# The first stage of a two-block transformer kernel: scale tiles ahead of the first products, shift tiles behind them

## The reference

```
mod = (silu(c) @ ada_w[0] + ada_b[0]).reshape(3, 3, D)          # shift, scale, gate for each sub-layer
def rms_norm(x, g): return x * rsqrt(mean(x * x) + eps) * g
h = rms_norm(x, g_pre) * (1 + scale) + shift                    # modulate_pre
g_, u = split(h @ w_in, 2)                                      # w_in 1024 x 5632
y = (silu(g_) * u) @ w_out                                      # w_out 2816 x 1024
x = x + 0.5 * gate * rms_norm(y, g_post)
```

## Time and profile before

| | us |
|---|---|
| median of 3 runs | 2181.11 |
| lowest and highest run | 2179.35, 2183.25 |
| profiled execution, its own time | 2186.3 |
| its span | 2184.4 |
| TensorE products busy in it | 2104.6 |

### The profile page before, as it was taken

The page is one execution under the profiler, slowest core; times in us unless marked ns, Lnnn a source line. Parts: engine busy times, 40 slices in busy tenths (PEclk is TensorE's granted clock), DMA queues, the critical chain, the costliest instruction groups (busy, mean ns, idle before and its releaser), DMA issues.

```text
span 2184.4 us, 39484 instructions
## 1 busy us (share of the span) xinstructions
PE 2104.6 (96%) x17016; PEld 2058.6 (94%) x17016; DVE 1586.2 (73%) x1948; ACT 1013.8 (46%) x1097; POOL 199.6 (9%) x333
## 2 busy tenths in 40 slices
PE   5999999999999998899999999999999999999998
PEld 5999999999999998699998999999999899999998
DVE  6887888787757876778888454768898646767655
ACT  3444545445433445644345453346344545336443
POOL 2110101111101101011101000001111000001000
PEclk9999999999879999999999999999999999999999
DMA  8898566995669953058975565446996655544663
GB/s 292 308 345 278 200 214 212 335 342 187 231 223 323 338 198 116 10 191 301 336 269 173 175 198 181 168 169 227 360 362 215 208 184 177 173 163 165 223 214 123
DMA packets 265389, 497.40 MB, mean 228 GB/s; under 512 B 17152, under 2 KB 146560, under 8 KB 264832
## 3 DMA queue, kind: packets, MB, share of 16 engines
q1 hardware_dynamic: 230192, 366.42, 50.2%
q0 software_dynamic: 35024, 128.47, 15.8%
HBM read 491.68 MB, written 1.05 MB: 226 GB/s over the span
## 4 chain that ended last, share of the span: by engine, by line
PE 81%; DVE 11%; ACT 4%; DMA 2%; issue 2%; SPq 0%; DVEq 0%; ACTq 0%
PE PA L505 8%; PE PA L507 8%; PE PA L506 8%; PE PY L505 7%; PE PB L505 7%; PE PY L507 7%; PE PB L507 7%; PE PY L506 7%; PE PB L506 7%; DVE wlo L1363 3%; ACT whi L1004 1%; DVE opA_lo L1452 1%; PE PA L585 1%; PE PA L536 1%; PE PB L901 1%
## 5 line engine op out<-in xcount | busy, mean ns | idle before, releaser
L1363 DVE TENSOR_TENSOR wlo<-raw,whi 128x2048 fp32r<-128x2048 f32 x335 | 768.0, 2302 | 346.2 <-ACT whi L1004 345.1
L1004 ACT ACTIVATE whi<-raw 128x2048 fp32r<-128x2048 f32 x335 | 636.5, 1907 | 493.8 <-DMA raw<-ffn_w_in 198.0
L505 PE MATMUL PY<-opB_hi,whi 128*128 128x256 f32 x1344 | 378.5, 282 | 9.1 <-DVE wlo L1363 8.3
L505 PE MATMUL PA<-opA_hi,whi 128*128 128x256 f32 x1312 | 371.8, 283 | 5.5 <-DVE opA_lo L1413 5.5
L506 PE MATMUL PY<-opB_lo,whi 128*128 128x256 f32 x1344 | 376.7, 280 | 0.0
L507 PE MATMUL PY<-opB_hi,wlo 128*128 128x256 f32 x1344 | 376.7, 280 | 0.0
L507 PE MATMUL PA<-opA_hi,wlo 128*128 128x256 f32 x1312 | 370.0, 282 | 0.0
L506 PE MATMUL PA<-opA_lo,whi 128*128 128x256 f32 x1312 | 369.0, 281 | 0.0
L505 PE MATMUL PB<-opA_hi,whi 128*128 128x256 f32 x1184 | 334.2, 282 | 1.1 <-DVE wlo L1363 1.0
L507 PE MATMUL PB<-opA_hi,wlo 128*128 128x256 f32 x1184 | 333.2, 281 | 0.0
L506 PE MATMUL PB<-opA_lo,whi 128*128 128x256 f32 x1184 | 332.2, 281 | 0.0
(11 more groups left out here) (311 smaller groups left out, 3629.5 us busy)
## 6 DMA issues: line engine op xcount, KB each, us to landing
raw<-ffn_w_in SPq DMA_DIRECT2D x176, 512.0 KB, 5.9
scr<-adat POOLq DMA_DIRECT2D x158, 512.0 KB, 6.4
raw<-w_in SPq DMA_DIRECT2D x144, 512.0 KB, 4.6
raw<-w_ff SPq DMA_DIRECT2D x128, 512.0 KB, 4.9
raw<-ffn_w_out SPq DMA_DIRECT2D x88, 512.0 KB, 5.1
adaw<-adat POOLq DMA_DIRECT2D x82, 512.0 KB, 6.2
raw<-w_branch SPq DMA_DIRECT2D x48, 512.0 KB, 4.6
raw<-a_w_in SPq DMA_DIRECT2D x24, 512.0 KB, 4.7
```

Source lines behind the costliest of these rows:

```text
L505: nc.tensor.matmul(o_, w1, rhs(xh), start=start, stop=False, skip_group_check=True)
L1004: AC(whi[slot][:, 0:w], raw[slot][:, 0:w], ACT.Copy).then_inc(hi_ready, 1)
L1363: TT(wlo[slot][:, 0:w], raw[slot][:, 0:w], whi[slot][:, 0:w].bitcast(F32), ALU.subtract).then_inc(lo_ready, 1)
```

## The change

The sync engine now loads the eight scale tiles first (tile 8 of the table is the first in order, `tile_of`), then chunk 0, x, chunk 1, four shift tiles, chunk 2, four shift tiles, chunk 3. Tiles 6 to 15 in the new order go into buffers of their own in a free area (`first_slab`), each with its own semaphore, so that none waits for a slab. VectorE makes the scale vector after eight tiles, then splits chunk 0, makes the low parts of the operand, splits chunk 1, multiplies four shift tiles and makes their half of the shift columns (mark `00.wide0`), splits chunk 2, and does the same with the other four (`00.wide1`). ScalarE makes all eight high parts before it rounds chunk 1, and rounds chunks 2 and 3 after the squares. TensorE's fillers come after tiles 3 to 8; another eight wait for chunk 0's high part.

`first_zgroups` replaces the two calls of `zgroup` in this stage: chunks 0 and 1 are multiplied with 256 columns, the high part of the operand first and the low part behind it; a block of 32 products with two columns (`shifts`) for chunk 0 stands behind chunk 1, the one for chunk 1 behind chunk 2, and `xnorm` behind that. Chunk 0 is counted as used after its block, chunks 1 and 2 together after the second. Chunks 2 and 3 keep 258 columns. VectorE waits for that count before it evacuates A and B. `ffn_due` of this stage starts its 40 tiles two chunks later and ends at the same place. A memset of GpSimd moves behind the first 16 tiles.

```diff
--- before.py
+++ after.py
@@ -201,7 +201,7 @@
         lo_ready = sem("lo_ready")
         multiplied = sem("multiplied")
         ada_ready = [sem(f"ada_ready{i}") for i in range(SLABS)]
-        first_ready = [sem(f"first_ready{i}") for i in range(SLABS)]
+        first_ready = [sem(f"first_ready{i}") for i in range(16)]
         ada_used = sem("ada_used")
         crow_in = sem("crow_in")
         crow_again = sem("crow_again")
@@ -303,17 +303,25 @@
             [(72 + 8 * b, V("ada_b", 72 + 8 * b, 8)) for b in range(9)] + [(160 + 8 * b, V("b_ada_2", 8 * b, 8)) for b in range(12)]
 
         nsa0 = RUN["nsa"][0]
-        SL = [g % SLABS for g in range(nsa0)] + [g % 2 for g in range(4)] + [(2 + g) % SLABS for g in range(256 - nsa0 - 4)]
+        SL = list(range(SLABS)) + [100 + g for g in range(SLABS, 16)] + [g % SLABS for g in range(16, nsa0)] + [g % 2 for g in range(4)] + [(2 + g) % SLABS for g in range(256 - nsa0 - 4)]
         BEFORE = [max([h for h in range(g) if SL[h] == SL[g]], default=-1) for g in range(256)]
 
         def ffn_due(name, p):
 
-            rn, a_ = RUN[name][1], 3 if name in ("ffn00", "ffn10") else 5
+            rn, a_ = RUN[name][1], 3 if name == "ffn10" else 5
             return min(rn, max(0, p - a_ + 1) * rn // (FFN_AT["in", FFN_STEPS - 1] - a_))
 
         def ff2_due(name, p):
             rn = RUN[name][1]
             return min(rn, max(0, p - 5) * rn // (FF2_AT["out", FF2_STEPS - 2] - 6))
+
+        def first_slab(g):
+
+            return slab[g] if g < SLABS else mix[:, D * (g - SLABS):D * (g - SLABS) + D]
+
+        def tile_of(g):
+
+            return g + 8 if g < 8 else g - 8 if g < 16 else g
 
         def ada_count(g):
             return sum(1 for h in range(16, g + 1) if SL[h] == SL[g])
@@ -391,9 +399,7 @@
             def first_ada(tiles):
 
                 for f in tiles:
-                    if f >= SLABS:
-                        sp.wait_ge(ada_used, f - SLABS + 1)
-                    sp.dma_start(slab[f % SLABS], I["adat"][f]).then_inc(first_ready[f % SLABS], 16)
+                    sp.dma_start(first_slab(f), I["adat"][tile_of(f)]).then_inc(first_ready[f], 16)
 
             def ffn(name, w_in, w_out):
                 c0 = CH[name]
@@ -415,7 +421,9 @@
                         for h in range(2):
                             chunk(p_ + h, src_ffn_in(w_in, j * 256, h))
                             if p_ + h == 0:
-                                first_ada(range(6, 16))
+                                sp.dma_start(x[:], I["x_fm"]).then_inc(x_in, 16)
+                            if p_ + h in (1, 2):
+                                first_ada(range(4 + 4 * (p_ + h), 8 + 4 * (p_ + h)))
                     else:
                         chunk(p_, src_out(w_out, j * 256))
 
@@ -427,8 +435,7 @@
             first_ada(range(0, 2))
             sp.dma_start(vec[:], I["vec"]).then_inc(vec_in, 16)
             sp.dma_start(base[:], I["t_base"]).then_inc(base_in, 16)
-            first_ada(range(2, 6))
-            sp.dma_start(x[:], I["x_fm"]).then_inc(x_in, 16)
+            first_ada(range(2, 8))
             ffn("ffn00", I["ffn_w_in"][0, 0], I["ffn_w_out"][0, 0])
             for n_, g in enumerate(CONV_ORDER):
                 for h in range(2):
@@ -550,6 +557,50 @@
                 for h in range(2):
                     zchunk(c + h, banks, tile, range(4 * h, 4 * h + 4), sub, hook if h == 0 else None)
 
+            def first_zgroups():
+
+                def z(c, banks):
+                    pe.wait_ge(lo_ready, c + 1)
+                    n = T if c < 2 else ZC
+                    for kk in range(4):
+                        k = 4 * (c % 2) + kk
+                        need(pe, "S", f"00.zhi{k}")
+                        for m in range(4):
+                            w_ = slice(tile_ffn_in(kk, m), tile_ffn_in(kk, m) + P)
+                            nc.tensor.matmul(banks[m][:, 0:n], whi[c][:, w_], wide[:, k, 0:n], start=k == 0, stop=False,
+                                             skip_group_check=True)
+                            nc.tensor.matmul(banks[m][:, 0:n], wlo[c][:, w_], wide[:, k, 0:n], start=False, stop=False,
+                                             skip_group_check=True)
+                        need(pe, "V", f"00.zlo{k}")
+                        for m in range(4):
+                            w_ = slice(tile_ffn_in(kk, m), tile_ffn_in(kk, m) + P)
+                            last = nc.tensor.matmul(banks[m][:, 0:T], whi[c][:, w_], opl["A"][:, k, :], start=False,
+                                                    stop=k == KT - 1, skip_group_check=True)
+                    return last
+
+                def shifts(c, banks):
+
+                    need(pe, "V", f"00.wide{c}")
+                    for kk in range(4):
+                        k = 4 * (c % 2) + kk
+                        for m in range(4):
+                            w_ = slice(tile_ffn_in(kk, m), tile_ffn_in(kk, m) + P)
+                            for w in (whi, wlo):
+                                last = nc.tensor.matmul(banks[m][:, T:ZC], w[c][:, w_], wide[:, k, T:ZC], start=False,
+                                                        stop=k == KT - 1, skip_group_check=True)
+                    return last
+
+                ab, y_ = zbanks("AB"), zbanks("Y")
+                z(0, ab)
+                z(1, ab)
+                shifts(0, ab).then_inc(multiplied, 1)
+                z(2, y_)
+                shifts(1, ab).then_inc(multiplied, 2)
+                xnorm("00")()
+                z(3, y_).then_inc(multiplied, 1)
+                for n_, j in (("A", 0), ("B", 0), ("Y", 1)):
+                    by(n_, "V", f"00.z{j}")
+
             def xnorm(sub):
 
                 def products():
@@ -597,6 +648,9 @@
                         if j == 0:
                             take("Y")
                         out_rows(p_, (0, 1), "B", 2 * (j % 2), j == 0, j == FFN_STEPS - 1, tag if j == FFN_STEPS - 1 else None)
+                    elif name == "ffn00" and j < 2:
+                        if j == 0:
+                            first_zgroups()
                     elif z and j < 2:
                         bufs = ("AB", "Y")[j]
                         for n_ in bufs:
@@ -660,10 +714,12 @@
 
 
             pe.wait_ge(base_in, 16)
-            for f in range(8, 17):
+            for f in range(3, 9):
                 pe.wait_ge(ada_used, f)
                 idle(6)
             need(pe, "V", "first.mod")
+            idle(8)
+            pe.wait_ge(hi_ready, 1)
             idle(8)
             ffn("ffn00", "00", True)
             by("Y", "V", "00.u7")
@@ -1162,11 +1218,10 @@
             need(act, "V", "first.mod")
             for k in range(KT):
                 S(AC(oph["A"][:, k, :], x[:, k, :], ACT.Copy, scale=A_("00")[:, k:k + 1]), f"00.zhi{k}")
-                if k == 3:
-                    prep_to(2)
+            prep_to(2)
             for k in range(KT):
                 S(AC(tmp8[:, k, :], x[:, k, :], ACT.Square), f"00.sq{k}")
-            prep_to(3)
+            prep_to(4)
             ffn("ffn00", "00", True)
             boundary("00", "01", CH["conv_in"], CH["conv_in"])
             c = CH["conv_in"]
@@ -1375,11 +1430,14 @@
                 while ran[0] < n:
                     g = ran[0]
                     if g < 16:
-                        dve.wait_ge(first_ready[g % SLABS], 16 * (g // SLABS + 1))
+                        dve.wait_ge(first_ready[g], 16)
+                        w = first_slab(g)
                     else:
                         dve.wait_ge(ada_ready[SL[g]], 16 * ada_count(g))
-                    nc.vector.tensor_tensor_reduce(slab[SL[g]], slab[SL[g]], crow[:], 1.0, 0.0, ALU.mult, ALU.add,
-                                                   accum_out=fresh[:, g % 64:g % 64 + 1]).then_inc(ada_used, 1)
+                        w = slab[SL[g]]
+                    f = tile_of(g) % 64
+                    nc.vector.tensor_tensor_reduce(w, w, crow[:], 1.0, 0.0, ALU.mult, ALU.add,
+                                                   accum_out=fresh[:, f:f + 1]).then_inc(ada_used, 1)
                     ran[0] += 1
 
             def mods(name):
@@ -1530,6 +1588,7 @@
                             if name == "ffn11":
                                 need(dve, "S", "csil1")
                             inverse(tag)
+                            dve.wait_ge(multiplied, c0 + (3 if name == "ffn00" else 2))
                             zevac(f"{tag}.j0", "AB")
                             seen["V", f"{tag}.z0"] = S.n
                             prep_to(p_ + 5)
@@ -1636,20 +1695,26 @@
                 mods(f"ff{l}")
 
             need(dve, "S", "csil0")
-            for f in range(16):
-                if f == 12:
-                    prep_to(1)
-                ada_to(f + 1)
+            ada_to(8)
             dve.wait_ge(vec_in, 16)
-            mods("first")
-            widened("00")
+            dve.wait_ge(ada_used, 8)
```

(18 more changed lines are left out.)

## The result

The changed kernel took 2185.23 us (median of 20 runs, 2179.28 to 2190.3). The kernel before, beside it on the same chip, took 2181.01 (20 runs). The ratio is 1.0022, 95% interval 1.0014 to 1.0030: slower by 4.2 us, where 3.8 us less were forecast. The profiled execution took 2187.71 us, its span 2185.7.

A forecast was written before the change was run, and what follows sets the result against it. With TensorE's products running 96% of the span, only its opening waits could be won: a 14.3 us earlier start, mostly lost to 7.0 of new products, 2.8 of low clock and longer waits, left 3.8: 2177.3 us, range 2175 to 2180.5.

The forecast's parts named there:

- That wait goes: VectorE's 3.93 us wait for chunk 5's data disappears, so the chain's end comes 3.5 us earlier.
- I take 3.8 off the median: Whole kernel: the opening's 3.8 us gain is subtracted from the median 2181.11 us, giving 2177.3.
- The second term, the clock: TensorE's two-column blocks: one half-clock spell of 3.4 us per block, 1.7 us lost each; bounds 0 to 6.8 us.
- The start at 26.1: TensorE's first real product comes at 26.1 us instead of 40.44, 14.3 us earlier.
- 0.11 us for a two-column product: TensorE's added blocks: 0.109 us per product, 3.5 us per block, 7.0 us in all.
- POOL's sum long done: POOL's sum for the norm ends at about 38.7 us and is no longer waited for.
- about 2 us of wait before the first output chunk: TensorE still waits some 2 us for chunk 6's split; its product moves from 77.96 to 74.45 us.
- the feed of tiles free of cost: POOL's later, denser tile feed, 344 GB/s against 331, is priced at 0.
- (a): Rival: the clock holds through TensorE's two-column blocks; gain 6.1 + 0.35 us, 2174.7 us; chance 12%.
- (b): Rival: two-column products cost only 0.056 us and drop no clock; gain 9.9 us, 2171.2 us; chance 6%.
- (c): Rival: chunk 5 still lands 12.3 us after its issue, nothing of the chain moves; 2181.0 us; chance 12%.
- (d): Rival: DMA can't give the tile feed 344 GB/s, stretching chunks 7 to 28; 2185.0 us at 324; chance 6%.

The follow-up runs named there:

- b1: The kernel before, unchanged, run and profiled a second time: 2180.66 us, ratio 0.9996.
- e4: The kernel before with only the changed kernel's due times for POOL's tiles: 2180.49 us, ratio 0.9999.
- e5: The kernel before with fewer TensorE fillers, four after each of nine tiles instead of six: 2185.15 us, ratio 1.0021 to the kernel before.
- after: The changed kernel itself, in its first batch and profile: 2185.23 us, ratio 1.0022 to the kernel before.
- e0: The changed kernel, unchanged, run and profiled a second time: 2185.52 us, ratio 1.0013 to the kernel before.
- e2: The changed kernel with each two-column block cut from 32 products to 4, leaving out most of the shift: 2177.28 us, ratio 0.9980 to the kernel before.
- e6: The changed kernel with POOL's additions for the norm held until VectorE has used twelve tiles: 2185.89 us, ratio 1.0018 to the kernel before.
- e12: The changed kernel with two-column products on weights of chunks 2 and 3, freeing chunks 0 and 1's buffers earlier: 2185.96 us, ratio 1.0014 to the kernel before.
- e1: The changed kernel with both blocks' 64 products 258 columns wide instead of two, results not the model's: 2181.80 us, ratio 0.9999 to the kernel before.
- e3: The changed kernel with the due times of POOL's tiles put back as before: 2185.42 us, ratio 1.0016 to the kernel before.
- e9: The changed kernel with the norm's products behind the first block and chunk 4's low part made early: 2186.56 us, ratio 1.0031 to the kernel before.
- e10: The changed kernel with two-column products spread among those of chunks 2 and 3, norm between, chunk 4's low part early: 2197.53 us, ratio 1.0072.
- e11: e9 with two-column products on weights of chunks 2 and 3, freeing chunks 0 and 1's buffers earlier: 2183.33 us, ratio 0.9996 to the kernel before.
- e8: The kernel before with both the new due times of POOL's tiles and fewer fillers: 2182.51 us, ratio 1.0012.

## Why the prediction was wrong

**What sets the opening.** In the table, chunk 5's high part starts 8.5 to 8.6 us behind the reciprocal in b1, e4, e5, after, e0, e2, e6 and e12. Where it is later, it waited for the load, 9.8 to 10.1 us behind its issue in e1, e3 and e9 (8.7 in e10, 12.3 in the first profile of before). e11 has neither: there the load is early and so is the norm, and VectorE reads out group 0's products when the second block has ended, at 55.6. e8, 9.4 behind, has no wait for a DMA: ScalarE's first high part of the next operand waited for TensorE's last products on chunk 3 (2.60 us, where b1 has 1.68 for VectorE), and these ran in the low clock shown above. In after, both ways begin at the same place, the end of the second block at 54.35. Before, in b1, they began at 51.2 (chunk 1 multiplied) and 52.3 (POOL's sum).

From chunk 5's high part on, ScalarE's order is rigid, the next high part comes 8.6 us later in every one of the profiles, so what is late there stays late for a while: the high part that starts at 268.35 in b1 starts at 271.67 in after, 264.74 in e2, 272.90 in e9, 281.75 in e10 and 267.49 in e11. Against b1, after is 2.2 us late at chunk 5's split (66.19 against 63.98), and e2 3.1 early, e9 5.0 late and e10 13.8 late; the medians against before stand at +4.2, -4.5, +4.7 and +15.7. The others fit less well: e1 0.2 early with +0.1, e3 2.6 late with +3.7, e12 3.2 late with +3.6, but e0 1.5 late with +3.8 and e11 1.5 early with +1.0.

**The step that failed** is "That wait goes. ... So the chain's end is 66.82 -> 63.3, 3.5 us earlier". The 3.93 us counted as won belonged to the one profiled run; in b1, e4 and e5 there are 1.19 us, set by ScalarE's order, and after has 1.20 of the same. This second bound was missing from the sum: it put the split 9.25 us behind the reciprocal, when VectorE's own list ends, and it starts 10.44 behind in b1 and in after, when ScalarE has rounded. With that the forecast's own reciprocal, 54.05 against 53.54 in b1, would have given a time slightly above before's. "I take 3.8 off the median" carried a wait of a run 5 us above the median into the median. The warning stood in the prediction: 2186.3 against 2179.35 to 2183.25.

**The second term, the clock, was mis-sized.** One spell for each block was counted, 2.3 us lost before the norm. The first took 6.8 us (3.4 lost) and stood wholly before the norm; the second, 3.4 us, began at 54.74, behind it, and a third at 78.6 followed TensorE's wait of 2.0 us. e1, which kept one spell of 3.4 us, prices the difference at 3.7 us. With the 0.64 us of the first block's wait this makes the reciprocal 55.75 instead of 54.05.

**A term that was missing** is VectorE beside POOL. The shift tiles' products took 1.75 us while POOL's additions ran and 1.21 when they had ended, and the first of the three small operations behind them 0.58 instead of 0.16: the columns of the first block were ready at 38.3, not 35.5. e6 shows that POOL is the cause. The Trainium skill says the same (SBUF — State Buffer, section "SBUF: two separate sides"): a VectorE operation with two inputs in SBUF and a GpSimd operation that reads it share a port pair that one of them holds for its whole instruction. The trace agrees: a product starts 1.15 us behind the last one alone and 1.68 beside POOL, and an addition of POOL takes 0.74 us alone (e6) and 1.54 beside a product. It cost the time nothing that the runs can tell.

**What was right.** The start at 26.1; 0.11 us for a two-column product (64 of them, 7 us); POOL's sum long done; about 2 us of wait before the first output chunk (its product came at 77.34, not 74.45, against 75.64 in b1); no TensorE wait between 95 and 232 us; the feed of tiles free of cost (e3, e4). Of the rivals, (a) asked for the clock to hold and (b) for cheap products: neither came true. (c), the load as late as before, did not apply (9.3 us or less instead of 12.3). (d), the tile feed, is excluded by e3; that its 2185.0 is nearly the measured time is chance. Two sums are slightly off by the prediction's own terms: the second block ends at 50.55 in (a) and 47.15 in (b), 0.3 later than stated, and 1.70 us over 32 to 36 records is 0.047 to 0.053, not 0.05 to 0.056. Neither bears on the outcome. None of them had a slower kernel by the end of the blocks, and that is what happened: the blocks' end is the release of chunk 1's buffer and the start of the norm, and it came at 54.35 instead of 51.2 and 52.3.

**What stays open.** Of after's 4.2 us, 2.2 are there at chunk 5. Of the rest, 1.1 more are there at chunk 32 (218.06 against 214.75), beside the spell at 78.6, which costs 1.7. What comes later can't be placed with one profile each: spells of low clock at 324, 857, 1505, 1673 and 1993 us come and go from one profile to the next. e6's profile has chunk 5's high part only 0.3 us behind b1's, and its median is 4.1 us above before all the same. e5, with the opening of b1, is as slow as after and shows the same spell near 321. Two profiles of the same changed kernel show how wide this scatter is: e0's span is 2180.3 us, after's 2185.7, and only 2.3 of these 5.4 us are there at 270 us. The profiled runs of e0, e5, e6 and e12 took 2.8 to 3.8 us less than their medians, so what makes these medians need not be in their profiles. A part of the cost may lie in how often TensorE's clock falls later on; no run here shows that, nor why the opening should move it. Not tried was a kernel that computes the model's shift with both the norm early and the buffers freed.

## What to carry to other kernels

A part of a product that is moved behind others keeps its weights' buffer: ask when the ring's slot is released and which load waits for that, before counting an earlier start as won. Take the waits that an edit is to remove from an execution whose time is near the median, or from two; a wait of several us in a run 5 us above it may be peculiar to that run, as 2.8 of these 5 us were here. And a start that comes 14 us earlier is worth nothing where the next stage hangs on something else: here the norm's product and the release of a weight buffer, both put behind the added products, came at 54.35 instead of 52.3 and 51.2.

## What the runs showed of the hardware

- Two-column products with a new 128x128 fp32r weight load each start 0.11 us apart at full clock and 0.21 at half (after). 258-column products in their place start 0.12 apart at full clock (e1).
- TensorE lost its full clock in each of the seven profiles with two blocks of 32 such products: in e6 without any wait before, in e9 at 38.5, 0.5 us into the block, behind a wait of 1.7 us. With 258 columns in the same place, behind a wait of 1.2 us, it kept it (e1). Mixed with 256-column products (32 among 50), the clock, which had fallen behind a wait of 2.6 us, stayed at 0.5 for 17.0 us on end (e10).
- The same wait of TensorE before the norm, 2.2 to 2.3 us, was followed by a clock of 0.5 in e8 and not in e5.
- VectorE's multiply-and-sum of 128x1024 took 1.75 us beside POOL's additions and 1.21 alone; POOL's six additions took 10.3 us, mostly beside it, against 8.95 in the earlier trace rows, where most of the time went to two that stood beside VectorE's splits (one took 2.60 us, in e6 one alone 0.74).
- The profiled run of one kernel can hold a load that lands 12.3 us after its issue where its next profile has it in 10.1 us or less (b1).
